# A two-layer block on one Trainium2 core: latents split straight from their banks, norm sums in a bank of their own, side blocks in another order, smaller first transfers

## What is computed

```python
def hybrid_layer(x, norm_g, w_in, b_f, q_norm_g, k_norm_g, w_pool, pool_scale, w_out):
    h = rms_norm(x, norm_g)
    proj = h @ w_in       # fq, fk, fv, fg, ff, px, pg, sq, sk, sv, sg
    fox_out = forgetting_attention(rms(fq), rms(fk), fv, log_sigmoid(ff + b_f)) * silu(fg)   # 8 heads
    pool_out = multiscale_pool(px, w_pool, pool_scale) * silu(pg)
    sb_out = stick_breaking_attention(sq, sk, sv) * silu(sg)                                 # 4 heads
    return x + concatenate([fox_out, pool_out, sb_out]) @ w_out

def second_block(x, p, ...):
    z = rmsnorm(x, mix_pre_norm) @ w_in        # latents q (256), kv (256), rope key (32), conv gates b, c, xv
    a = mla(latent q, latent kv, rope key)     # rmsnorm of each latent, w_uq / w_ukv, rope, 8-head attention
    c = b * causal_conv3(c_gate * xv)
    m = concatenate([rmsnorm(a, attn_group_norm), rmsnorm(c, conv_group_norm)])
    x = x + rmsnorm(m @ w_out, mix_post_norm)
    h = rmsnorm(x, ffn_pre_norm)
    x = x + rmsnorm((silu(h @ w_gate) * (h @ w_up)) @ w_down, ffn_post_norm)
    e = rmsnorm(p @ w_ple_proj, ple_norm)
    return x + sigmoid(x @ w_ple_gate) * e
```

## Time and profile before

| | before |
|---|---|
| median of 3 runs | 927.1 us (926.96 to 928.42) |
| the profiled execution | 926.5 us, of it span 924.7 us |
| TensorE busy | 908.5 us (98%) |
| VectorE, ScalarE, GpSimd busy | 397.3, 332.3, 467.6 us |
| mean granted TensorE clock | 0.997 of full speed |
| read from memory | 78.8 MB, 88 GB/s over the span |

### The profile page before, as it was taken

How to read it: one execution, slowest core, us unless ns; L and a number is a source line. 1 busy time by engine, 2 the same in 40 slices (tenths; PEclk the granted TensorE clock), 3 DMA queues, 4 the chain that set the end, 5 groups by cost and what they waited for, 6 DMA issues and landing times.

```text
span 924.7 us, 12710 instructions
## 1 busy us (share of the span) xinstructions
PE 908.5 (98%) x4540; PEld 740.2 (80%) x4540; DVE 397.3 (43%) x661; ACT 332.3 (36%) x663; POOL 467.6 (51%) x374
## 2 busy tenths in 40 slices
PE   8999999999999999999989999999999999999998
PEld 7889877676779988876667988888888888888787
DVE  1664463568634474786547441111111122222562
ACT  3333413454326102556637722222222233223421
POOL 7967674321435866833125374444444444555343
PEclk9999999999999999999999999999999999999999
DMA  6432232100102322221011232322232323222213
GB/s 213 137 113 93 98 106 70 46 24 23 69 25 90 132 96 85 98 92 42 5 47 68 92 137 94 110 91 91 96 108 91 114 91 108 97 91 91 71 66 114
DMA packets 28202, 81.55 MB, mean 88 GB/s; under 512 B 6000, under 2 KB 8432, under 8 KB 28160
## 3 DMA queue, kind: packets, MB, share of 16 engines
q1 hardware_dynamic: 24000, 78.65, 24.6%
q10 hardware_dynamic: 4160, 2.32, 1.0%
HBM read 78.83 MB, written 2.10 MB: 88 GB/s over the span
## 4 chain that ended last, share of the span: by engine, by line
PE 88%; DVE 7%; issue 2%; POOL 1%; ACT 1%; DMA 0%; DVEq 0%; POOLq 0%; ACTq 0%
PE bank L485 25%; PE bank L487 25%; PE bank L486 25%; PE bank L677 4%; PE bank L542 3%; PE bank L700 2%; PE bank L785 2%; DVE aT_lo L1683 1%; POOL w_lo L439 1%; DVE arena L1683 1%; DVE PT L1683 1%; DVE PT L2036 0%; DMA x<-in_x 0%; DVE PT L1904 0%; DVE aT_lo L1715 0%
## 5 line engine op out<-in xcount | busy, mean ns | idle before, releaser
L439 POOL TENSOR_TENSOR w_lo<-raw,w_hi 128x512 fp32r<-128x512 f32 x282 | 380.8, 1372 | 218.9 <-ACT w_hi L1233 212.8
L485 PE MATMUL bank<-w_hi,aT_hi 128*128 128x512 f32 (+4 forms) x600 | 228.6, 381 | 6.0 <-DVEq L2106 2.5
L485 PE MATMUL bank<-aT_hi,w_hi 128*128 128x512 f32 (+1 forms) x600 | 230.6, 384 | 1.5 <-ACT arena L1233 1.4
L487 PE MATMUL bank<-aT_hi,w_lo 128*128 128x512 f32 (+1 forms) x600 | 226.9, 378 | 0.0
L486 PE MATMUL bank<-aT_lo,w_hi 128*128 128x512 f32 (+1 forms) x600 | 226.8, 378 | 0.0
L487 PE MATMUL bank<-w_hi,aT_lo 128*128 128x512 f32 (+4 forms) x600 | 222.7, 371 | 0.0
L486 PE MATMUL bank<-w_lo,aT_hi 128*128 128x512 f32 (+4 forms) x600 | 222.6, 371 | 0.0
L432 POOL TENSOR_SCALAR w_hi<-raw 128x1024 fp32r<-128x1024 f32 x71 | 79.8, 1123 | 218.7 <-PE bank L487 179.9
L1233 ACT ACTIVATE w_hi<-raw 128x1024 fp32r<-128x1024 f32 x70 | 74.2, 1061 | 238.8 <-PE bank L487 221.1
L485 PEld LDWEIGHTS bank<-w_hi,aT_hi 128*128 128x128 f32 x600 | 113.4, 189 | 27.4 <-DVEq L2106 2.9
L485 PEld LDWEIGHTS bank<-aT_hi,w_hi 128*128 128x128 f32 x600 | 113.0, 188 | 22.6 <-POOL w_lo L439 1.7
(11 more groups left out here) (210 smaller groups left out, 832.7 us busy)
## 6 DMA issues: line engine op xcount, KB each, us to landing
raw<-in_weights SPq DMA_DIRECT2D x141, 512.0 KB, 3.2
x<-in_x SPq DMA_DIRECT2D x4, 512.0 KB, 7.5
y_out<-x SPq DMA_DIRECT2D x7, 256.0 KB, 3.8
g_post<-in_gains ACTq DMA_DIRECT2D x3, 512.0 KB, 3.2
raw<-in_weights SPq DMA_DIRECT2D x2, 256.0 KB, 5.2
arena<-in_pt ACTq DMA_DIRECT2D x1, 512.0 KB, 4.2
y_out<-x SPq DMA_DIRECT2D x2, 128.0 KB, 1.9
wpool<-in_wpool ACTq DMA_DIRECT2D x1, 128.0 KB, 5.5
```

Of the source, the lines that this page charges most:

```text
L439: lo = nc.gpsimd.tensor_tensor(w_lo[:, s, at], raw[:, r, at], w_hi[:, s, at].bitcast(F32), ALU.subtract)
L485: mm(out, st_hi, mv_hi, start=start, stop=False)
L487: return mm(out, st_lo, mv_hi, start=False, stop=stop)
```

## The change

Start: x's first transfer is cut in two of 128 columns each, with a half of the first weight chunk behind each of them; chunk 1 is split by GpSimd in halves as well. The gain comes as eight rows of 128 and is turned by TensorE and copied out of the bank by VectorE. The constants' transfers are issued behind ScalarE's third split. There are 9 + 4 + 6 turns of the identity instead of 14 + 10. For blocks 0 and 1 of fq TensorE makes the high by high products of all four row tiles first, turns column blocks, and then makes the others.

First attention: sk 1 is built from blocks 4, 5, 0, 1, 2, 3, 6, 7; `mix_high`/`mix_low` of blocks 4, 5, 0, 1 are at steps 25/26 to 28/29; the tail pieces use (4, 5), 0 and 1.

Latents: all four blocks are split from their banks into `lat_parts` within conv block 1; `latT` and `lat_first` are gone. ScalarE makes conv high parts 4 to 6 after the last conv matmul, VectorE low parts 4 and 5 ahead of the rotation, 6 and 7 behind it.

Norm sums: `ssa` lies in bank 3. ScalarE copies embedding row 2 ahead of `pair_hi(0)`.

```diff
+SK_LAST = (4, 5, 0, 1, 2, 3, 6, 7)
...
-            tiles["latT", i] = (n % 8, "act" if i else "dve", None)
+            tiles["latT", i] = (n % 8, "dve", None)
...
-            tiles["ssa", 0] = (2, "dve", None)
+            tiles["ssa", 0] = (3, "dve", None)
...
+        lat_parts = nc.alloc_sbuf_tensor_at("lat_parts", [P, 2, 4, S], F32R, offset=arena_at + 4 * 8200)
...
-        q2T = ar(8196, MLA_H, S)
+        q2T = ar(8200, MLA_H, S)
...
-            for j in range(KD // 2):
-                load_x(j)
-                if j == 0:
-                    sp_.dma_start(raw[:, 0, 0:S], w_d[0, :, 0:S]).then_inc(w_first_in, 16)
-                    sp_.dma_start(raw[:, 0, S:CW], w_d[0, :, S:CW]).then_inc(raw_in[0], 16)
-                elif j < RAW:
+            load_x(slice(0, P), x_first_in)
+            sp_.dma_start(raw[:, 0, 0:S], w_d[0, :, 0:S]).then_inc(w_first_in, 16)
+            load_x(slice(P, 2 * P), x_in[0])
+            sp_.dma_start(raw[:, 0, S:CW], w_d[0, :, S:CW]).then_inc(raw_in[0], 16)
+            for j in range(1, KD // 2):
+                load_x(slice(j * 2 * P, (j + 1) * 2 * P), x_in[j])
+                if j < RAW:
                     load(j, True, j)
...
-                    if a == 0:
+                    if a < RAW:
                         split_halves(a, a)
...
+            def fq_first(k, turns):
+                at = slice(k * S, (k + 1) * S)
+                pe.wait_ge(mix_hi, k + 1)
+                pe.wait_ge(hi_made if k else w_half, 1)
+                for t in range(T):
+                    mm(tbank(("fq", t))[:, :], left(k, t)[0], w_hi[:, 0, at], start=(k == 0), stop=False)
+                for n in turns:
+                    turn_column(n)
+                left_ready(1)
+                for t in range(T):
+                    mm(tbank(("fq", t))[:, :], left(k, t)[1], w_hi[:, 0, at], start=False, stop=False)
+                pe.wait_ge(w_split if k else w_half, 1 if k else 2)
+                for t in range(T):
+                    last = mm(tbank(("fq", t))[:, :], left(k, t)[0], w_lo[:, 0, at], start=False, stop=False)
+                if k:
+                    last.then_inc(w_used, 1)
...
-            keep_awake(14)
-            turn_columns(0)
-            keep_awake(10)
+            keep_awake(9)
+            pe.wait_ge(g_col_in, 16)
+            nc.tensor.transpose(bank[2][:, 0:KD], g_row[:, :], ident[0:KD, 0:KD]).then_inc(g_turned, 1)
+            keep_awake(4)
+            turn_column(0)
+            keep_awake(6)
+            fq_first(0, (1,))
+            fq_first(1, (2, 3))
...
-                k = m % KD
+                n = m % KD
+                k = SK_LAST[n] if key == ("sk", 1) else n
...
-                elif key == ("sk", 1) and k < 6:
+                elif key == ("sk", 1) and n < 5:
                     last.then_inc(sk_read, 1)
...
-                n, ks = ((0, (0, 1)), (2, (4,)), (2, (5,)))[j]
+                n, ks = ((2, (4, 5)), (0, (0,)), (0, (1,)))[j]
...
-                        st = left(k, t) if k else (lat_first[:, 0, at], lat_first[:, 1, at])
+                        st = lat_parts[:, 0, k, at], lat_parts[:, 1, k, at]
...
-            act_.dma_start(g_col[:, :], gains_d[0, 0, :].rearrange("(k p) -> p k", p=P),
-                            allow_slow_non_contiguous=True).then_inc(g_col_in, 16)
+            act_.dma_start(g_row[:, :], gains_d[0, 0, :].rearrange("(k p) -> k p", p=P)).then_inc(g_col_in, 16)
...
             for k in range(KD):
+                if k == 3:
+                    act_.dma_start(cols[:, :], cols_d).then_inc(const_in, 16)
+                    act_.dma_start(wpool[:, :, :], wpool_d).then_inc(const_in, 16)
+                    act_.dma_start(pos_i[:, :], pos_d).then_inc(const_in, 16)
...
-                for at, b in ((27, 0), (28, 1), (30, 4), (31, 5)):
+                for at, b in ((25, 4), (26, 5), (27, 0), (28, 1)):
                     if m == at:
-                        act_.wait_ge(sk_read, b + 1)
-                        act_.wait_ge(pv_drained, min(b, 1) + 1)
+                        act_.wait_ge(sk_read, SK_LAST.index(b) + 1)
+                        if b < FOX_H // 2:
+                            act_.wait_ge(pv_drained, b + 1)
                         mix_high(b)
...
-                    for i in range(1, 4):
-                        split_hi(aT_hi[:, i, :], latT[:, i, :], col("gq2", i) if i < 2 else col("gkv2", i - 2))
+                    for i in range(3):
+                        split_hi(aT_hi[:, 4 + i, :], y[:, i, :], col("gc", i))
...
-                    full(act_, ("latT", 0))
-                    split_hi(lat_first[:, 0, :], tbank(("latT", 0))[:, :], col("gq2"))
-                    for i in range(1, 4):
+                    for i in range(4):
                         full(act_, ("latT", i))
-                        drain(("latT", i), copy(latT[:, i, :], tbank(("latT", i))[:, :]))
+                        split_hi(lat_parts[:, 0, i, :], tbank(("latT", i))[:, :],
+                                 col("gq2", i) if i < 2 else col("gkv2", i - 2))
...
-            for j in range(4):
-                split_hi(aT_hi[:, 4 + j, :], y[:, j, :], col("gc", j))
+            split_hi(aT_hi[:, 7, :], y[:, 3, :], col("gc", 3))
...
+            ple_out(2)
             pair_hi(0)
-            ple_out(2)
...
-            dve.wait_ge(g_col_in, 16)
+            dve.wait_ge(g_turned, 1)
+            V.tensor_copy(g_col[:, :], bank[2][:, 0:KD]).then_inc(g_made, 1)
...
-                for at, b in ((28, 0), (29, 1), (31, 4), (32, 5)):
+                for at, b in ((26, 4), (27, 5), (28, 0), (29, 1)):
...
                 if j == 3:
-                    dve.wait_ge(w_used, CH["conv"] + 12)
-                    for i in range(1, 4):
-                        split_lo(None, aT_lo[:, i, :], latT[:, i, :], aT_hi[:, i, :].bitcast(F32),
-                                 col("gq2", i) if i < 2 else col("gkv2", i - 2))
+                    conv_lo(0)
+                    conv_lo(1)
...
-                    split_lo(("latT", 0), lat_first[:, 1, :], tbank(("latT", 0))[:, :],
-                             lat_first[:, 0, :].bitcast(F32), col("gq2"))
+                    for i in range(4):
+                        split_lo(("latT", i), lat_parts[:, 1, i, :], tbank(("latT", i))[:, :],
+                                 lat_parts[:, 0, i, :].bitcast(F32), col("gq2", i) if i < 2 else col("gkv2", i - 2))
...
-            for j in range(4):
-                split_lo(None, aT_lo[:, 4 + j, :], y[:, j, :], aT_hi[:, 4 + j, :].bitcast(F32), col("gc", j))
+            conv_lo(2)
+            conv_lo(3)
```

More of the change, by code:

```diff
@@ L282, in hybrid_kernel @@
         rope_t = view(PTf, 0, 4, MLA_H * HALF)
-        y2 = [ar(5124 + t * D, D) for t in range(T - 1)] + [ar(18436, D)]
+        y2 = [ar(5124 + t * D, D) for t in range(T - 1)] + [ar(18440, D)]
         act = ar(0, NF, S)
@@ L414, in split_halves @@
                 for half in range(2):
-                    pool.wait_ge(raw_in[s] if half else w_first_in, 16)
+                    pool.wait_ge(w_first_in if c + half == 0 else raw_in[s], 16)
                     at = slice(half * 512, (half + 1) * 512)
@@ L601, in _ @@
             pe.wait_ge(ident_made, 2)
-            keep_awake(14)
-            turn_columns(0)
-            keep_awake(10)
-            for j, ks in pairs:
-                if j == 0:
-                    left_ready(1)
-                    pe.wait_ge(w_half, 2)
-                    for t in range(T):
-                        fq_step(t, 0)
-                    turn_columns(1)
-                    left_ready(1)
-                    chunk(CH["fq"])
-                    for t in range(T):
-                        fq_step(t, 1)
-                else:
-                    left_ready(2)
-                    chunk(CH["fq"] + j)
-                    for t in range(T):
-                        if t == 2 and j < 3:
-                            turn_columns(j + 1)
-                        for k in ks:
-                            fq_step(t, k)
+            keep_awake(9)
[6 more added lines that the diff above has]
+            fq_first(1, (2, 3))
+            left_ready(1)
+            pe.wait_ge(w_half, 4)
+            for t in range(T):
+                fq_step(t, 2)
+            turn_column(4)
+            turn_column(5)
+            left_ready(1)
+            chunk(CH["fq"] + 1)
+            for t in range(T):
+                fq_step(t, 3)
+            for j, ks in pairs[2:]:
+                left_ready(2)
+                chunk(CH["fq"] + j)
+                for t in range(T):
+                    if t == 2 and j < 3:
+                        turn_column(2 * j + 2)
+                        turn_column(2 * j + 3)
+                    for k in ks:
+                        fq_step(t, k)
             weights_moving([("fv", t) for t in range(T)], group4("fv"), S)
@@ L946, in _ @@
                     at = slice(k * 512 + i * P, k * 512 + (i + 1) * P)
```

(13 more changed lines are left out.)

48 lines of the change are left out of this document (24 added, 24 removed).

## The result

**Result.** The changed kernel takes 917.34 us (median of five runs, 917.24 to 917.61) against 927.1 for the kernel before: a ratio of 0.9898, 95% interval 0.9884 to 0.9911. Forecast were 918.9 and a range of 916.6 to 922.0. The profiled execution took 917.55 us, 915.8 of it span; the one before took 926.5 and 924.7, with the busy times of the earlier trace rows. Of the five runs of the kernel before beside the changed one, four took 926.85 to 928.42 us and one took 1302.84, which no other run of any kernel comes near.

What follows compares the result with a forecast made beforehand. TensorE bounds the kernel, busy 908.5 of 924.7 us, so only its idle time and low clock can be won. Gains 1.5 + 2.1 + 2.3 + 2.3 = 8.2; 926.5 - 8.2 = 918.3, plus 0.6: 918.9 us, range 916.6 to 922.0.

Steps and rivals of the forecast that it cites:

- The start: Kernel start: first matmul at 6.3 us instead of 8.28, less column 1's turns now behind it; gain 1.5 us.
- rival 3: Kernel start: gain row lands at 5.2, first matmuls at the low clock, no gain or a loss; 920.4 to 922.0, chance 0.10.
- The tail: End of first attention: earlier gate splits and reordered blocks leave no side piece waiting, values start 2.1 us earlier.
- Latents: Latents and second attention: VectorE has fewer splits there, so TensorE's waits of 0.3 and 1.85 us go; gain 2.3 us.
- the rsqrt: Before the second attention's first maximum: late next, ending near 405.5; gain 0 if it takes the wait's place.
- rival 2: Behind the out projection: TensorE waits about 2 us in pieces and the clock falls again; costs 1.6 us, 920.5, chance 0.16.
- the 1.85 us wait at 405.60 was not: Ahead of the second attention's scores: claimed this TensorE wait was not followed by a low clock.
- Norm sums: Out projection to feed-forward: bank 3 removes the 2.47 us wait and 1.6 us of low clock; 2.3 us kept, ends 1.2 and 4.1.
- The collision with the first update: VectorE's first row update: earlier GpSimd embedding-weight splits meet it and cost 0.4 + 1.1 us, so the chain gains 2.3, not 3.7.
- the multiply of 2.33 us: VectorE's row 2 at 497.2: meeting GpSimd's splits, it lasts 2.33 instead of 1.28 us; GpSimd was ahead by 0.06.
- rival 1: VectorE's first row update slips past GpSimd's splits unhit; the last part gains 3.7 us, 917.5, chance 0.12.
- The moved copy: Embedding row 2's copy ahead of the pair's ScalarE splits: removes a 1.36 us wait at 508.25, worth 0 to 0.3, taken as 0.

Runs made afterwards that it cites:

- the one with the wide turn: The changed kernel with the gain row's turn over 128 moving columns in place of 8: 918.93 us, ratio 0.9912 to the kernel before.
- the kernel before with its falls taken away: The kernel before with 16 identity turns ahead of the second attention's scores wait and 21 ahead of the bank 2 wait: 925.24 us, ratio 0.9979.

## Why the prediction was right, and where it was off

**The start**, forecast 1.5: 1.4 by medians. But the composition was not the forecast one, and that the size fits is luck. I had the first matmul at 6.3 with the clock up near 5; it was 6.81 in the changed kernel, 6.40 to 6.8 in the others but the one with the wide turn, with a clock that may rise as late as 7.9. Some 0.6 come from the first matmuls; 0.8 more from two short stops at 286 and 326 that are missing, the first of them with the code of the new start, less 0.3 at 492; nothing in a reading of the change could give that. The price of rival 3 was partly paid, in the profiled execution.

**The tail**, forecast 2.1: 2.2 in the change and alone, the values at 209.59, 2.7 sooner than before with 0.5 of that from the start. The turns and the scale came as written down.

**Latents**, forecast 2.3: 2.4, in the change and alone. The first maximum is at 402.26, and the rsqrt didn't take the wait's place. What failed is a step that I had used against rival 2: "the 1.85 us wait at 405.60 was not" followed by a low clock. In two kernels that kept this wait, it was.

**Norm sums**, forecast 2.3: 2.5 alone, 3.2 in the change, within the ends of 1.2 and 4.1. The collision with the first update came as forecast, for 1.1 us where the sum took 1.4 off for it. The step that failed is that one of before's meetings, the multiply of 2.33 us, would stay: a race by 0.06 us at 497.2 that I quoted for rival 1 and then left out of the sum. The kernel with ScalarE delayed by a copy shows what it turns on.

**The moved copy**, taken as 0: 0, shown by taking it back.

**The rest.** The forecast sum was 8.2 us, the spans differ by 8.9, the medians by 9.8. The 0.7 between the first two is mostly the race behind the norm sums. The 0.8 to 0.9 between the last two is the difference of two draws: the profile of before had one fall and stood 0.6 under its median, that of after had a late clock rise and stood 0.2 over its own. Against the kernel before with its falls taken away (925.24) the change is worth 7.9 us. Rival 2 asked for a fall behind the out projection; the profiles of all kernels that have neither wait show none, with 1.2 us as the longest stop left there.

## What to carry to other kernels

A wait of TensorE can cost more than it lasts, and not every execution shows it: look at the single times for steps before trusting one profile, and fill a wait that must stay with turns. Where VectorE's chain sets the end, list its instructions with both inputs in SBUF and hold GpSimd's work behind them with a semaphore; at meetings decided by 0.05 us the order is luck, and a later ScalarE can be faster. When single parts are timed, judge each in a kernel where the other waits are already gone.

## What was not expected of the hardware

- A fall of the granted clock to 0.50 came behind stops of 1.9 and 2.5 us in some executions and in others not. With the stops filled with turns, 4.6 us of spread became 0.5 in eleven of twelve runs; the twelfth still had a fall.
- The start's rise of the clock came anywhere between 5.0 and 7.9 us, up to 2.4 apart in two kernels with the same start.
- Short idle spots of some 0.35 us, in which an engine stands between a finished semaphore instruction and its next one with all inputs ready, recur at one place of an engine's program and go when code elsewhere is added: the one of VectorE at 286 (0.50 with the usual gap) stops TensorE for 0.3 us in all nine profiled kernels without the gain row and in none of the five with it. What causes them wasn't tried.
